# Second mixer of a two-block transformer: global heads first, then banded heads, with panels and half of the output projection between the attention's steps

## The chip, the cores and the metric

One core of one Trainium2 chip. The metric is the device time of one execution in microseconds. TensorE (PE), VectorE (DVE), ScalarE (ACT), GpSimd (POOL) and the load queue of SyncE (SP) run their own instruction streams in order and meet at semaphores.

## The reference

Two transformer blocks on 512 tokens of width 1024, in fp32. The change concerns the mixer of the second block:

```python
h = rms_norm(x, norm_mix_pre[l])
qa, ka, va, qb, kb, vb = jnp.split(h @ w_in[l], SPLITS, axis=-1)
qa = apply_rope(rms_norm(qa.reshape(B, S, 8, 64), q_norm_a[l]), ang_axial)
ka = apply_rope(rms_norm(ka.reshape(B, S, 2, 64), k_norm_a[l]), ang_axial)
out_a = global_attention(qa, ka, va)          # all 512 keys
qb, kb = apply_rope(qb, ang_1d), apply_rope(kb, ang_1d)
out_b = window_attention(qb, kb, vb, sink_b[l])   # |key - query| <= 128, one sink logit per head
mixed = jnp.concatenate([rms_norm(out_a, group_norm_a[l]),
                         rms_norm(out_b, group_norm_b[l])], axis=-1) @ w_out[l]
x = x + rms_norm(mixed, norm_mix_post[l])
```

Eight global heads (a) share two key heads, eight banded heads (b) likewise.

## The kernel before

Activations lie transposed, features on partitions and 512 tokens in the free dimension. Each fp32 product is made of three matmuls of rounded parts: high by high, low by high, high by low (lines 710 to 712). A weight **unit** is a 128 x 1024 panel: SyncE loads it into one of four raw slots, GpSimd splits it into high and low part (`split`, lines 595 and 597) in one of two slots, TensorE uses it in eight **chunks** of three matmuls. A split waits until the unit two before it is used up (`unit_done`).

The second mixer, in TensorE's order:
- twelve panels (units U_B2) for keys, queries and values, a and b by turns. Query panels hold head j and head j + 4 of their kind. Between their chunks stand, for a: the fp32 sum of squares per head (`sum_a`, line 808), then VectorE's `head_norm` (reciprocal L1917, scaling L1919), the fp32 rotation (`turn_a`, L811), VectorE's `rope` (L1925 multiply, L1929, L1932 add), and high and low part; for b the rotation alone. The factor of the norm over all features, `r_all`, multiplies the panels' results.
- attention over 16 heads, in pairs a, a, b, b. A step is one key block of 128: an a head has four, a b head four and one for the sink. For each step `scores_t` makes transposed scores plus the shift by the row maximum (L856 to L864), ScalarE takes exponentials twice, GpSimd makes the low part of the probabilities (L632), and two steps later `values_mm` adds to the output (L885 to L887). Row maxima come from a second set of scores (`scores`, L841), which TensorE makes for head h + 1 during steps 0 and 1 of head h; VectorE's `maxes` (L1949) reads them, and in step 2 `diagonal` (L1963, for b after L1959) writes the shift as four diagonal matrices. `output` (L1978, L1981) divides a pair's result one step after ScalarE has copied it out.
- `w_out_2`: eight units of the output projection, each for 128 output features, over all eight chunks c of the normalized heads; chunks 0 to 3 are a, 4 to 7 b, in two banks. The two group norms' factors are taken afterwards, in `join` (L2437, L2440, L2442). GpSimd's splits go on ahead; during the attention GpSimd makes only low parts.

Banks: two for scores, three for transposed scores, two for outputs. During `fox_slot`, in the first block's mixer (580 to 740 us of the span), another attention stands chunk by chunk between panels, with one bank for scores and two for transposed scores.

## Time and profile before

| | us |
|---|---|
| median of 3 runs | 2176.59 |
| lowest, highest | 2175.07, 2177.75 |
| the profiled execution | 2175.67 |
| its span | 2173.6 |
| TensorE busy | 2004.6 |
| GpSimd busy | 1226.0 |
| VectorE busy | 1105.3 |
| ScalarE busy | 505.0 |

Times below are microseconds from the start of the span. The busy time of TensorE counts each matmul to its modelled end, and matmuls overlap, so the distance of their starts is the better measure of work. A wait in the trace is put down to the releaser that came last.

### The profile page before, as it was taken

What the parts mean: (1) busy time and instruction counts of PE and PEld (TensorE: products, weight loads), DVE (VectorE), ACT (ScalarE), POOL (GpSimd) and SP (SyncE); (2) the same over time, 40 slices, a digit from 0 to 9 for tenths busy, and PEclk for the clock granted to TensorE, in tenths of its full rate; (3) what the DMA queues carried; (4) which work ended last, traced back from release to release, by engine and by line L of the source; (5) the groups of instructions that cost most, each with busy time, mean ns of one, the idle gap of its engine ahead of it and who ended that gap; (6) DMA issues with size and microseconds to landing.
All of it is one profiled execution on the core that took longest, in us unless ns stands there. A gap on an engine that the chain in (4) does not pass through costs nothing.

```text
span 2173.6 us, 25282 instructions
## 1 busy us (share of the span) xinstructions
PE 2004.6 (92%) x8955; PEld 1623.3 (75%) x8955; DVE 1105.3 (51%) x1308; ACT 505.0 (23%) x916; POOL 1226.0 (56%) x752
## 2 busy tenths in 40 slices
PE   7999999789989899889999999998888869999996
PEld 5888888467767687678778888876676748888884
DVE  5333430557676467666653332039778684333104
ACT  3111100344334342350111110022365321111001
POOL 4666666336645545436666666664445456666661
PEclk9999999889999999999999999999999979999998
DMA  4333323212211223102323333233100113333220
GB/s 150 97 97 96 97 96 88 78 49 78 68 49 50 59 59 87 49 1 83 92 88 96 96 96 98 96 90 84 49 0 1 39 49 97 96 96 96 97 87 39
DMA packets 259808, 163.83 MB, mean 75 GB/s; under 512 B 30380, under 2 KB 249582, under 8 KB 259614
## 3 DMA queue, kind: packets, MB, share of 16 engines
q1 hardware_dynamic: 258080, 157.90, 24.8%
q10 hardware_dynamic: 1662, 5.06, 0.7%
q8 instruction: 41, 0.67, 0.1%
q14 instruction: 25, 0.20, 0.0%
HBM read 160.81 MB, written 2.13 MB: 75 GB/s over the span
## 4 chain that ended last, share of the span: by engine, by line
PE 77%; DVE 14%; ACT 3%; issue 2%; POOL 2%; ACTq 1%; DMA 0%; POOLq 0%; DVEq 0%; SPq 0%
PE bank L710 12%; PE bank L711 12%; PE bank L712 12%; PE bank L778 5%; PE bank L777 5%; PE bank L779 5%; PE bank L971 3%; PE bank L972 3%; PE bank L973 3%; DVE work L1978 2%; PE bank L841 2%; DVE work L1917 1%; PE bank L1176 1%; PE bank L1177 1%; PE bank L1178 1%
## 5 line engine op out<-in xcount | busy, mean ns | idle before, releaser
L597 POOL TENSOR_TENSOR w_lo<-raw,w_hi 128x1024 fp32r<-128x1024 f32 x298 | 746.1, 2504 | 24.9
L595 POOL TENSOR_SCALAR w_hi<-raw 128x1024 fp32r<-128x1024 f32 x298 | 320.5, 1075 | 711.9 <-PE bank L712 340.9
L710 PE MATMUL bank<-u_hi,w_hi 128*128 128x512 f32 x1184 | 476.3, 402 | 28.8 <-DVE u_lo L1866 19.1
L711 PE MATMUL bank<-u_lo,w_hi 128*128 128x512 f32 x1184 | 465.4, 393 | 0.0
L712 PE MATMUL bank<-u_hi,w_lo 128*128 128x512 f32 x1184 | 465.0, 393 | 0.0
L710 PEld LDWEIGHTS bank<-u_hi,w_hi 128*128 128x128 f32 x1184 | 224.6, 190 | 91.3 <-issue 25.5
L711 PEld LDWEIGHTS bank<-u_lo,w_hi 128*128 128x128 f32 x1184 | 225.0, 190 | 49.5 <-issue 4.7
L712 PEld LDWEIGHTS bank<-u_hi,w_lo 128*128 128x128 f32 x1184 | 224.9, 190 | 47.1
L1892 DVE TENSOR_TENSOR work<-bank,work 128x512 f32<-128x512 f32 x66 | 45.6, 691 | 285.1 <-PE bank L712 285.1
L779 PE MATMUL bank<-hid_hi,w_lo 128*128 (+1 forms) x480 | 186.9, 389 | 0.0
L778 PE MATMUL bank<-hid_lo,w_hi 128*128 (+1 forms) x480 | 186.9, 389 | 0.0
L777 PE MATMUL bank<-hid_hi,w_hi 128*128 (+1 forms) x480 | 186.9, 389 | 0.0
L971 PE MATMUL bank<-u_hi,w_hi 128*128 128x512 f32 x384 | 158.3, 412 | 2.4 <-ACT work L1328 1.1
L1897 DVE TENSOR_TENSOR hid_lo<-work,hid_hi 128x512 f32 (+1 forms) x66 | 123.1, 1865 | 59.4 <-ACT hid_hi L1365 59.4
L972 PE MATMUL bank<-u_lo,w_hi 128*128 128x512 f32 x384 | 151.5, 395 | 0.0
L973 PE MATMUL bank<-u_hi,w_lo 128*128 128x512 f32 x384 | 151.4, 394 | 0.0
L1365 ACT ACTIVATE hid_hi<-work 128x512 f32 (+1 forms) x66 | 41.8, 633 | 360.2 <-DVE work L1895 360.2
L1949 DVE TENSOR_REDUCE rowmax<-bank 128x1 f32<-128x512 f32 (+3 forms) x144 | 72.7, 525 | 90.4 <-PE bank L841 89.6
L632 POOL TENSOR_TENSOR p_pl<-work,p_ph 128x512 fp32r<-128x512 f32 (+2 forms) x64 | 73.4, 1157 | 70.4 <-ACT work L1416 70.3
L1912 DVE SCALAR_TENSOR_TENSOR hT<-bank,hT 128x512 f32<-128x512 f32 x16 | 11.0, 688 | 199.2 <-PE bank L800 199.2
L777 PEld LDWEIGHTS bank<-hid_hi,w_hi 128*128 128x128 f32 x480 | 90.2, 188 | 18.8
L779 PEld LDWEIGHTS bank<-hid_hi,w_lo 128*128 128x128 f32 x480 | 90.2, 188 | 18.6
(463 smaller groups left out, 3293.7 us busy)
## 6 DMA issues: line engine op xcount, KB each, us to landing
raw<-in_w_in SPq DMA_DIRECT2D x52, 512.0 KB, 3.7
raw<-in_ffn_w_gate SPq DMA_DIRECT2D x44, 512.0 KB, 3.8
raw<-in_ffn_w_up SPq DMA_DIRECT2D x44, 512.0 KB, 3.7
raw<-in_ffn_w_down SPq DMA_DIRECT2D x44, 512.0 KB, 3.5
raw<-in_w_gate SPq DMA_DIRECT2D x22, 512.0 KB, 3.7
raw<-in_w_up SPq DMA_DIRECT2D x22, 512.0 KB, 3.7
raw<-in_w_down SPq DMA_DIRECT2D x22, 512.0 KB, 3.7
raw<-in_w_branch SPq DMA_DIRECT2D x12, 512.0 KB, 3.4
```

The lines of the kernel that those rows point to most:

```text
L595: pool.tensor_scalar(w_hi[:, s, :], raw[:, k, :], 1.0, 1.0, ALU.mult, ALU.mult).then_inc(hi_done, 1)
L597: pool.tensor_tensor(w_lo[:, s, :], raw[:, k, :], w_hi[:, s, :].bitcast(F32), ALU.subtract).then_inc(split_ready, 1)
L710: pe.matmul(outs[:, 0:n], wh, rhs_hi[:, c, :], start=(c == 0), stop=False)
L711: pe.matmul(outs[:, 0:n], wh, rhs_lo[:, c, :], start=False, stop=False)
L712: last = pe.matmul(outs[:, 0:n], wl, rhs_hi[:, c, :], start=False, stop=(c == KC - 1))
L777: pe.matmul(bank[m][:], wh, hid_hi[:, j, :], start=start, stop=False)
L778: pe.matmul(bank[m][:], wh, hid_lo[:, j, :], start=False, stop=False)
L779: last = pe.matmul(bank[m][:], wl, hid_hi[:, j, :], start=False, stop=stop)
L971: pe.matmul(o, wh, rhs_hi[:, c, :], start=(c == 0), stop=False)
L972: pe.matmul(o, wh, rhs_lo[:, c, :], start=False, stop=False)
L973: last = pe.matmul(o, wl, rhs_hi[:, c, :], start=False, stop=(c == KC - 1))
L1897: dve.tensor_tensor(hid_lo[:, f, :], W[8 + k], hid_hi[:, f, :].bitcast(F32), ALU.subtract).then_inc(f_lo, 1)
```

## The change

- Order: `b2_heads` now holds the eight a heads, then the eight b heads, so o2T's chunk g is pair g.
- Panels stand in the order of B2_PANELS. Six (ka, qa0, va, qa1, kb, qa2) come before the attention, six (qa3, qb0, qb1, vb, qb2, qb3) are **fillers**: a generator gives one chunk at a time, four between head 0's scores, then five per head.
- The output projection's units cover 256 output features of one group. The four of group a (A_HALF, 32 chunks) are fillers too, the four of group b (`w_out_b`) follow the attention. VectorE's `half_out` multiplies the first half by its group's factor during the attention; `join` adds the second.
- Scores have one bank, transposed scores two, banks 4 and 5 serve the fillers, bank 1 the turns and sums (AUX). Maxima move to steps 1 and 2, the diagonal to step 3.
- Norms, turns and low parts of the later heads are put at fixed steps of the loop (`hooks` on TensorE, `later` on VectorE and ScalarE). ScalarE makes two extra square roots inside it, each followed by `load_exp`.
- Low parts of the probabilities get three rotating places (`prob_lo`) for four fixed ones. GpSimd splits ten units between them.

Tables, orders and the splits:

```diff
+B2_PANELS = "ka", "qa0", "va", "qa1", "kb", "qa2", "qa3", "qb0", "qb1", "vb", "qb2", "qb3"
+B2_BANK = dict(zip(B2_PANELS, (2, 3, 4, 5, 4, 5, 4, 5, 4, 5, 4, 5)))
+B2_AHEAD = 6
...
+        b2_ph = at("b2_ph", [P, TT * S], b2a, F32R)
+        b2a += 8192
+        prob_lo = at("prob_lo", [P, 3, S], work_at + 7 * 2048, F32R)
+        for st in (ast, bst):
+            st |= {"ph": b2_ph, "pl": None, "off": SPREAD}
...
+        S_ORDER = "va", "ka", "qa0", "qa1", "kb", "qa2", "qa3", "qb0", "qb1", "vb", "qb2", "qb3"
+        ROPE_ORDER = "a0", "a1", "a2", "b0", "a3", "a4", "b1", "b2", "b3", "b4"
...
+        B2_BANKS = (0,), (2, 3), (6, 7), None
+        FIRST_FILL = 4
+
+        A_HALF = [(m, c) for m in range(2) for c in range(3)] + [(0, 3), (1, 3)]
+        A_HALF += [(m, c) for m in range(2, KC) for c in range(4)]
+
+        def fill_step(k):
+
+            head, i = (k - FIRST_FILL) // 5, (0, 1, 1, 2, 2)[(k - FIRST_FILL) % 5]
+            return (4 * head if head < 8 else 32 + 5 * (head - 8)) + i
...
-            low_parts(A_B2, b2_heads)
-            for u in range(U_WO2 + SPL, U_GU3 + SPL):
+            emptied = {fill_step(KC * k + KC - 1): U_B2 + B2_AHEAD + k for k in range(10)}
+            for x, step in enumerate(b2_steps):
+                if step[2] is not None:
+                    low_part(A_B2, b2_heads, step)
+                if x in emptied:
+                    one(emptied[x] + SPL)
+            for u in range(U_WO2 + 4 + SPL, U_GU3 + SPL):
...
         b2_heads = []
         for j in range(4):
             for job in pair(ast, whole, q=qa2[j]):
-                b2_heads.append(job | {"q_ready": S_B2 + (LAST_A if j == 3 else 2 * j + 3) + 1, "v_ready": S_B2 + V_A + 1})
+                b2_heads.append(job | {"q_ready": s_no(f"qa{j}") + 1, "v_ready": s_no("va") + 1})
+        for j in range(4):
             for job in pair(bst, window, q=qb2[j], extra=lambda *a, j=j: band(qb2[j][0], *a), extra_t=band_t, sinks=j):
-                b2_heads.append(job | {"q_ready": S_B2 + (LAST_B if j == 3 else 2 * j + 2) + 1, "v_ready": S_B2 + V_B + 1})
+                b2_heads.append(job | {"q_ready": s_no(f"qb{j}") + 1, "v_ready": s_no("vb") + 1})
         b2_steps = steps_of(b2_heads)
         b2_ends = [last_step(b2_steps, 2 * g + 1) for g in range(KC)]
```

TensorE:

```diff
...
-                for p in range(4, 12):
-                    j = (p - 4) // 2
-                    if p % 2 == 0:
-                        pe.wait_ge(qa_raw, j + 1)
-                    else:
-                        pe.wait_ge(r_raw, RR_B2 + j + 1)
-                    panel(u + p, p % SPL, 2 + p % 4, U, hooks(p))
-                attend(A_B2, b2_heads, part="rest", hooks={
-                    3: lambda: (pe.wait_ge(r_out, R_B2 + 10), values(VR_B2 + 1, 5, W[1]))})
...
+            def out_mm(b, slot, m, c, hi):
+                j, o = c % 4, bank[b][:]
+                a = j * 2 * P + m % 2 * P
+                pe.matmul(o, w_hi[:, slot, a:a + P], hi[:, j, :], start=j == 0, stop=False)
+                pe.matmul(o, w_hi[:, slot, a:a + P], ou_lo[:, c, :], start=False, stop=False)
+                return pe.matmul(o, w_lo[:, slot, a:a + P], hi[:, j, :], start=False, stop=j == 3)
+
+            def fillers():
+
...
+                for name in B2_PANELS[B2_AHEAD:]:
+                    for c in b2_panel(name):
+                        yield
+                        if c == 0:
+                            bank_free(name)
+                for m, c in A_HALF:
+                    yield
+                    u = U_WO2 + m // 2
+                    if c == 0:
+                        pe.wait_ge(split_ready, u + 1)
...
+                    pe.wait_ge(g_lo, c + 1)
+                    last = out_mm(Q_BANK + m % 2, u % SPL, m, c, oua_hi)
+                    if c == 3:
+                        last.then_inc(unit_done if m % 2 else g_half, 1)
+
...
+                for c in b2_panel("qa1"):
+                    if c == 2:
+                        sum_a(0, 6)
+                    if c == 5:
+                        pe.wait_ge(h_std, H_B2 + 1)
+                        sum_a(1, 6)
+                pe.wait_ge(v_raw, VR_B2 + 1)
+                for c in b2_panel("kb"):
+                    if c == 1:
+                        pe.wait_ge(qa_raw, 1)
+                        values(VR_B2, 2, W[0])
+                    if c == 4:
+                        turn_a(0, 7)
+                    if c == 6:
+                        pe.wait_ge(h_std, H_B2 + 2)
+                        sum_a(2, 6)
+                pe.wait_ge(qa_raw, 3)
+                for c in b2_panel("qa2"):
+                    if c == 6:
+                        pe.wait_ge(r_out, rope_no("a0") + 1)
+                        turn_a(1, 7)
+                fill = fillers()
+                next(fill)
+                scores, scores_t, values_mm = attention(A_B2, b2_heads, B2_BANKS)
+                for qt in range(TT):
+                    scores(0, qt)
+                    go_on(fill, 1)
+                    if qt == 0:
+                        pe.wait_ge(h_std, H_B2 + 3)
+                        sum_a(3, 6)
...
+                hooks = {
+                    2: lambda: (pe.wait_ge(h_std, H_B2 + 4), turn_a(2)),
+                    3: lambda: aux_free("a2", lambda: turn_b(0)),
+                    5: lambda: aux_free("b0", lambda: turn_a(3)),
+                    9: lambda: aux_free("a3", lambda: sum_a(4, AUX)),
+                    13: lambda: turn_a(4),
+                    17: lambda: aux_free("a4", lambda: turn_b(1)),
+                    20: lambda: aux_free("b1", lambda: turn_b(2)),
+                    27: values_b,
+                    32: lambda: (pe.wait_ge(s_lo, s_no("vb") + 1), turn_b(3)),
+                    40: group_sum_a,
+                    44: lambda: (pe.wait_ge(g_std, 1), turn_b(4)),
+                }
+                for x, (h, i, kb, t, b) in enumerate(b2_steps):
+                    if x in hooks:
+                        hooks[x]()
+                    scores_t(h, i, kb, t)
+                    more = h + 1 < len(b2_heads) and i in (1, 2)
+                    if i <= 2:
+                        go_on(fill, 1)
+                    if more:
+                        scores(h + 1, 2 * i - 2)
+                    if x >= PV_LAG and b2_steps[x - PV_LAG][2] is not None:
+                        h_, i_, kb_, t_, b_ = b2_steps[x - PV_LAG]
+                        values_mm(h_, i_, kb_, b_)
+                    if i in (1, 2):
+                        go_on(fill, 1)
+                    if more:
+                        scores(h + 1, 2 * i - 1)
+                for h, i, kb, t, b in b2_steps[-PV_LAG:]:
+                    if kb is not None:
+                        values_mm(h, i, kb, b)
+                for _ in fill:
...
+                for c in range(4, 7):
+                    pe.wait_ge(g_lo, c + 1)
+                    for m in range(4):
+                        out_mm(banks[m], (u + m // 2) % SPL, m, c, oub_hi)
+                pe.wait_ge(g_lo, 8)
+                for m in range(4):
+                    out_mm(banks[m], (u + m // 2) % SPL, m, 7, oub_hi).then_inc(unit_done if m % 2 else g_half, 1)
+                    if m == 1:
+                        pe.wait_ge(a_o, A_B2[3] + 16)
+                        pe.wait_ge(g_add, 6)
+                        pe.matmul(bank[6][:], ones, raw_x[:, 0, :], start=True, stop=True).then_inc(g_sum, 1)
+                for m in range(4, KC):
+                    v = u + m // 2
+                    pe.wait_ge(split_ready, v + 1)
+                    if m >= 6:
+                        pe.wait_ge(g_part, KC + m - 5)
+                    for c in range(4, 8):
+                        last = out_mm(banks[m], v % SPL, m, c, oub_hi)
+                    last.then_inc(unit_done if m % 2 else g_half, 1)
+                sum_total(N_POST, 7)
+            w_out_b()
```

VectorE:

```diff
...
                 raw_a_of(0)
+                raw_a_of(1)
+                raw_v_of(0)
+                norm_a(0)
+                raw_a_of(2)
+                value_low(s_no("va"), ast, 2)
                 dve.wait_ge(ld_tab, 16)
...
+                turn_a(0, 7)
+                norm_a(1)
+                low_a(0)
+                scale_tables()
+                turn_a(1, 7)
+                low_a(1)
+                raw_a_of(3)
...
+                def half_out(m):
+                    if m % 2:
+                        dve.wait_ge(unit_done, U_WO2 + m // 2 + 1)
...
+                    dve.tensor_tensor(mo[:, m, :], bank[Q_BANK + m % 2][:], W[0], ALU.mult).then_inc(g_part, 1)
+                first = {b2_ends[g] + PV_LAG + 6: [lambda g=g: group_low(g)] for g in range(KC - 1)}
+                later = {
+                    0: [lambda: norm_a(2)],
+                    2: [lambda: turn_a(2)],
+                    3: [lambda: (low_a(2), dve.wait_ge(tab_scaled, 1), turn_b(0))],
+                    4: [lambda: norm_a(3)],
+                    6: [lambda: (low_b(0), turn_a(3), raw_a_of(4))],
+                    8: [lambda: low_a(3)],
+                    12: [lambda: norm_a(4)],
+                    14: [lambda: turn_a(4)],
+                    16: [lambda: low_a(4)],
+                    17: [lambda: turn_b(1)],
+                    18: [lambda: low_b(1)],
+                    20: [lambda: turn_b(2)],
+                    22: [lambda: low_b(2)],
+                    25: [lambda: raw_v_of(1)],
+                    28: [lambda: value_low(s_no("vb"), bst, AUX)],
+                    33: [lambda: turn_b(3)],
+                    36: [lambda: low_b(3)],
+                    41: [lambda: factor(0)],
+                    45: [lambda: turn_b(4)],
+                    47: [lambda: low_b(4)],
+                }
+                for m in range(KC):
+                    x = fill_step(KC * (len(B2_PANELS) - B2_AHEAD) + A_HALF.index((m, 3))) + 1
+                    first.setdefault(max(42, x), []).append(lambda m=m: half_out(m))
+                maxes, diagonal, output = attention(A_B2, b2_heads, lambda r, g: o2T[r, g, :], B2_BANKS)
+                for qt in range(TT):
+                    maxes(0, qt)
+                diagonal(0)
+                for x in range(len(b2_steps) + PV_LAG + 3):
+                    h, i = b2_steps[x][:2] if x < len(b2_steps) else (len(b2_heads), 0)
+                    for step in first.get(x, []):
+                        step()
+                    if h + 1 < len(b2_heads) and i in (1, 2):
+                        maxes(h + 1, 2 * i - 2)
+                        maxes(h + 1, 2 * i - 1)
+                    if h + 1 < len(b2_heads) and i == 3:
+                        diagonal(h + 1)
+                    if x - PV_LAG - 2 in b2_ends:
+                        output(b2_ends.index(x - PV_LAG - 2))
+                    for step in later.get(x, []):
+                        step()
                 group_low(KC - 1)
+                factor(1)
```

## Rows read from the trace of the kernel before

**Rows 1.** The page, part 1: busy time, share of the span, instructions of each engine.

```profile
PE 2004.6 (92%) x8955; PEld 1623.3 (75%) x8955; DVE 1105.3 (51%) x1308; ACT 505.0 (23%) x916; POOL 1226.0 (56%) x752
```

**Rows 2.** Busy time of each engine by stage (columns: PE, PEld, DVE, ACT, POOL, clock).

```profile
580.00:740.00 160.00, 145.46 (x683) 115.48 (x684) 102.75 (x120) 62.30 (x126) 85.42 (x67) 0.97 0.18 48
...
1551.00:1701.00 150.00, 128.41 (x667) 106.75 (x666) 112.09 (x167) 91.35 (x188) 76.81 (x66) 0.98 0.01 4
1701.00:1752.00 51.00, 47.60 (x196) 37.47 (x196) 39.92 (x35) 8.95 (x15) 24.89 (x15) 0.97 0.23 68
1752.00:1767.00 15.00, 2.08 (x2) 0.50 (x2) 10.88 (x9) 2.60 (x5) 5.77 (x4) 0.58 0.18 52
1767.00:1785.00 18.00, 13.36 (x26) 7.82 (x27) 17.45 (x18) 8.64 (x15) 10.69 (x7) 0.50 0.00 1
```

**Rows 3.** Timeline of TensorE: start and end of the loop, end of the projection.

```profile
1551.51 0.39 PE L856 MATMUL bank<-q2ah,a_k0h 128*128 128x512 f32 x1
...
1700.09 0.39 PE L889 MATMUL bank<-b_k1h,zero_r 128*128 128x512 f32 x1
...
1750.89 0.39 PE L1282 MATMUL bank<-ou_hi,w_lo 128*128 128x512 f32 x1
```

**Rows 4.** Waits of TensorE, 1551 to 1701 (waiter, releaser: us, times, longest).

```profile
PE bank L841 <- DVE rowmax L1949: 7.9, 6, 1.4
...
PE bank L885 <- POOL p_pl L632: 5.3, 7, 1.1
...
PE bank L864 <- DVE shift L1963: 3.0, 2, 1.5
PE bank L884 <- POOL p_pl L632: 2.7, 1, 2.7
```

**Rows 5.** Waits of TensorE, 580 to 740, attention of the first mixer.

```profile
PE bank L856 <- ACT work L1416: 4.5, 3, 1.7
PE bank L808 <- ACT work L1378: 4.4, 1, 4.4
...
PE bank L841 <- DVE rowmax L1949: 3.6, 7, 0.6
```

**Rows 6.** Timeline of TensorE: an fp32 sum and the chunks behind it.

```profile
1479.15 1.12 PE L808 MATMUL bank<-work,const 128*128 128x512 f32 x2 [2.15 <-ACT work L1768]
...
1480.35 0.40 PE L711 MATMUL bank<-u_lo,w_hi 128*128 128x512 f32 x1
...
1482.41 0.39 PE L711 MATMUL bank<-u_lo,w_hi 128*128 128x512 f32 x1
```

**Rows 7.** Operations on the raw heads of the projection (ns, min/median/max).

```profile
L1919 DVE SCALAR_TENSOR_TENSOR raw_a<-raw_a,gain,work x5: 750/752/2058, 1486.3 to 1539.6; 128x512 f32<-128x512 f32 x5
L1925 DVE TENSOR_TENSOR raw_a<-raw_a,tab x5: 686/1524/2760, 1491.2 to 1555.8; 128x512 f32<-128x512 f32 x5
L1932 DVE TENSOR_TENSOR raw_a<-raw_a,turn_tmp x5: 692/986/2085, 1492.6 to 1557.9; 128x512 f32<-128x512 f32 x5
```

**Rows 8.** Groups of VectorE, 1551 to 1701 (busy us, mean ns, idle before).

```profile
L1978 DVE RECIPROCAL work<-work 128x512 f32<-128x512 f32 x7 | 23.5, 3353 | 7.2 <-ACT work L1427 7.1
L1949 DVE TENSOR_REDUCE rowmax<-bank 128x1 f32<-128x512 f32 x28 | 18.0, 685 | 7.9 <-PE bank L841 7.9
...
L1959 DVE TENSOR_SCALAR negmax<-rowmax,sink 128x4 f32<-128x4 f32 x8 | 6.7, 837 | 0.2
```

**Rows 9.** Timeline of VectorE: four diagonals beside GpSimd, and alone.

```profile
1584.40 1.62 DVE L1963 TENSOR_SCALAR shift<-const,rowmax 128x128 fp32r<-128x128 f32 x4
...
1610.88 0.88 DVE L1963 TENSOR_SCALAR shift<-const,negmax 128x128 fp32r<-128x128 f32 x4
```

**Rows 10.** Timeline of VectorE: the factor r_all, the last low part, last squares.

```profile
1474.43 3.29 DVE L1842 RECIPROCAL work<-work 128x512 f32<-128x512 f32 x1
...
1707.93 0.75 DVE L2419 SCALAR_TENSOR_TENSOR ou_lo<-o2T,gain,ou_hi 128x512 fp32r<-128x512 f32 x1 [1.38 <-ACT turn_tmp L1811]
...
1755.40 1.47 DVE L1877 TENSOR_TENSOR work<-work 128x512 f32<-128x512 f32 x2
```

**Rows 11.** Groups of GpSimd, 1445 to 1560.

```profile
L597 POOL TENSOR_TENSOR w_lo<-raw,w_hi 128x1024 fp32r<-128x1024 f32 x14 | 36.1, 2581 | 1.2
```

More of the change, by code:

```diff
@@ L254, in two_blocks @@
         tab_scaled, qa_raw, g_part = sem("tab_scaled"), sem("qa_raw"), sem("g_part")
+        g_sq, g_add, g_sum, g_std, g_rec, g_hi, g_lo, g_half = (
+            sem("g_" + n) for n in ("sq", "add", "sum", "std", "rec", "hi", "lo", "half"))
         c_two, g_raw = sem("c_two"), sem("g_raw")
@@ L1220, in first_key, with turn_a, turn_b, sum_a @@
+            def turn_a(a, b=AUX):
+                pe.wait_ge(h_out, H_B2 + a + 1)
+                rotate(b, raw_x[:, X_OF[a], :])
+            def turn_b(j):
+                pe.wait_ge(r_raw, RR_B2 + j + 1)
+                rotate(AUX, raw_x[:, 2 + j % 2, :])
+            def sum_a(a, b):
+                head_sum(H_B2 + a, b, HEAD_SQ[a], blk64)
+            def mixer_in():
                 def first_key(c):
@@ new lines, in mixer_in @@
+                exps, output = attention(A_B2, b2_heads, lambda r, g: o2T[r, g, :], B2_BANKS)
+                ends = {last_step(b2_steps, h): h for h in range(len(b2_heads))}
+                for x in range(len(b2_steps) + PV_LAG + 1):
+                    if x in first:
+                        group_high(first[x])
+                    if x < len(b2_steps):
+                        exps(*b2_steps[x])
+                    if x in later:
+                        later[x]()
+                    if x - PV_LAG - 1 in ends:
+                        output(ends[x - PV_LAG - 1])
@@ L2391, in mixer_in @@
-                last.then_inc(tab_scaled, 1)
-                raw_a_of(1)
-                norm_a(0)
-                dve.wait_ge(tab_scaled, 1)
-                turn_b(0)
-                dve.wait_ge(h_out, H_B2 + 1)
-                turn_a(0)
-                low_b(0)
-                for j in range(1, 5):
-                    norm_a(j)
-                    if j < 4:
-                        raw_a_of(j + 1)
-                    else:
-                        raw_v_of(0)
-                    turn_b(j)
-                    low_a(j - 1)
-                    dve.wait_ge(h_out, H_B2 + j + 1)
-                    if j < 4:
-                        turn_a(j)
-                        low_b(j)
@@ L2425, in mixer_in @@
-                attend(A_B2, b2_heads, put, part="first")
-                hooks = {b2_ends[g] + PV_LAG + 6: lambda g=g: group_low(g) for g in range(KC - 1)}
-                hooks |= {0: lambda: value_low(S_B2 + V_A, ast, 6), 1: lambda: raw_v_of(1), 2: lambda: turn_a(4),
-                          3: lambda: (low_b(4), low_a(4)), 5: lambda: value_low(S_B2 + V_B, bst, 5)}
-                attend(A_B2, b2_heads, put, part="rest", hooks=hooks)
+                raw_a_of(1)
+                raw_v_of(0)
```

405 lines of the change are left out of this document (211 added, 194 removed).

## The prediction

> **What bounds the kernel now.** The page gives TensorE 92% of the span [rows 1]. The stage table comes next, because the change touches only 1453 to 1757: twelve panels of the second mixer's projection until 1551, then the attention loop, then the output projection [rows 2]. In the loop TensorE is called 128.4 us busy of 150 and VectorE 112.1; in the projection TensorE is 47.6 of 51. Landmarks: the loop's first transposed score starts at 1551.51, its last matmul at 1700.09, so it ends near 1700.3; the last projection matmul starts at 1750.89 [rows 3]. The loop is 148.8 us long. Its waits on TensorE come to 18.9 us, 12.7% of it: row maxima, the low parts of the probabilities, the shift [rows 4]. So TensorE bounds the stage, with VectorE close behind and handshakes between them. What interleaving could win is those waits, plus what the panel stage loses. VectorE's 112.1 of 150 us limit the win.
>
> **Work that moves.** Matmuls of 512 columns follow each other every 0.228 us (nine from 1480.35 to 1482.41), so one chunk (three matmuls) is 0.68 us; an fp32 sum or turn between them takes 1.20 - 0.23, about 0.9 us [rows 6]. No matmul is added or removed: 96 panel chunks, 64 output chunks, the same attention. Into the loop move 76 chunks (48 of panels and 32 of the output's first half, less four issued just before it), 51.8 us, and ten sums and turns, 9 us (turn_a(2) to (4), sum_a(4), turn_b(0) to (4), the group sum). The old loop without its waits and without the 2% that a clock of 0.98 cost [rows 2] is 148.8 - 18.9 - 3 = 127 us, its small handshakes included. New loop: 127 + 52 + 9 = 188 us of TensorE work.
>
> **Its start.** Until the factor r_all (reciprocal from 1474.43, 3.29 us: 1477.7 [rows 10]) nothing changes. From there VectorE sets the pace: three products (1.8) and the wait for the first root, 1480.8; norm_a(0), a reciprocal and a scaling (3.35 + 0.75, the scaling up to 2.06 [rows 7, 8]), 1484.9; raw_a_of(2) behind panel qa1, 1486.4; value_low behind its transposes, 1488.6; turn_a(0), 1492.0; norm_a(1), 1496.1; low_a(0) and the tables 2.7 to 4, turn_a(1) 2.0, its high and low part 1.3: about 1503. Head 0's four scores, four chunks and a sum take 5.5: the loop starts at 1508.5 (within 1.5), 43 us earlier than before.
>
> **Waits in the new loop.** Four edits make it tighter. Maxima are taken at i = 1 and 2 and the diagonal at i = 3, before at 0, 1 and 2: between the last score of the next head and the matmul that needs its shift TensorE now has two short steps, 2.3 us. The scores have one bank for two. The hooks put a norm (4.1 us), turns and low parts between maxima, and three TensorE hooks wait for just these. In the banded half an output factor (sum, reciprocal, product: 0.6 + 3.4 + 0.6 at the pace at which they follow each other) falls at i = 2, ahead of the diagonal. VectorE's pieces: a 512-wide maximum 0.69 and a head's reciprocal 3.35, the negated maxima 0.84 with what they wait for [rows 8]; four diagonals 0.88 alone, 1.62 beside GpSimd [rows 9]; a turn 2.0 alone, to 3.5 when its multiply and add meet GpSimd (686 to 2760 ns, 692 to 2085 [rows 7]).
> One place in full, step 13. VectorE takes the last maximum 0.7 after its score; at step 11 it makes the diagonal (1.0) and output(0) (4.0), at 12 norm_a(4) (4.1): 9.8 us after the score. TensorE has 1.6 of work at step 11 and 2.3 at step 12, then turn_a(4) asks for the norm: it idles 5.9 us, 7 if the scaling meets GpSimd. Counted likewise in order: step 1, 1.6 to 2; step 3 (turn_b(0) behind turn_a(2)) 2.7 to 3.4; step 5 (turn_a(3) behind low_a(2), which waits for ScalarE, and norm_a(3)) 4 to 5.5; step 8 (shift behind low_b(0), turn_a(3), raw_a_of(4)) 3.2 to 5; step 16, 2.1 to 3.4; steps 21, 24 and 32, 2.2 to 5.6. Global half: 22 to 32 us. Banded half: three times 0.45 + 4.6 + 0.5 to 1.2 + 0.9 to 1.6 against 2.3, 12 to 17 us; steps 41 to 43 (root and table load, factor(0), half_out) 1 to 3; the other diagonals 0 to 3. In all 36 to 55 us. I take 40, near the lower end, since the 127 above already hold the usual handshakes. The loop is then 228 us and ends at 1736.5.
>
> **Low parts and splits.** GpSimd needs about 3.5 us for a split (the low part alone 2.58 [rows 11]); ten of them now stand between low parts of probabilities. Each chunk group lasts 8/5 of a head, over 17 us, so a split is ready in time; a low part behind it is 1.3 us late at worst, and the products lag two steps. Nothing is taken for it; exposed each time it is 10 x 1.3. The queue of loads (SyncE) is filled long before: no cost. ScalarE's extra copies lie in its idle time.
> At this place the Trainium skill speaks, "SBUF — State Buffer", section "Who interferes with whom": a VectorE instruction with two SBUF inputs and a GpSimd one that reads SBUF exclude each other for a whole instruction. The trace agrees with it, 686 against 2760 ns for one multiply [rows 7]; by that rule alone the upper ends above would be the usual case and the loop 15 us longer.
>
> **The tail.** Before: 1700.3 to the last square's sum, 1755.40 + 1.47 = 1756.9 [rows 10]: 56.6 us. After: twelve chunks (8.2 us) cover the last head's factor, whose low part starts 7.6 us after the last matmul and ends 8.4 after it [rows 10]; then two chunks 1.4, sum 0.9, root 0.6, reciprocal 3.4: 14.8. Eight joins with square sums of 1.9 us each, 15.5, and some 4 us of meeting GpSimd's four splits: 34.5 us (31 to 40). VectorE, not TensorE (24 us), bounds it. Gain 22.1 us. What follows (root, residual, next feed-forward, at a clock of 0.5 [rows 2]) is the same.
> Sum against the profiled execution's 2175.7 us: break-even is a loop end of 1756.9 - 34.5 = 1722.4. 1736.5 is 14.1 us later: 2189.8. The median of the runs, 2176.6, stands 0.9 above the profiled one, so 2190 to the full microsecond. I forecast slower, 2190, own range 2182 to 2198.
>
> **Rivals.**
> (1) No change. If TensorE waits the same share as before, 12.7%, the loop is 188/0.873 = 215 us and ends at 1723.8: 2177. For it: VectorE's busy share hardly changes (75% before; after, 112.1 and some 43 of moved operations, 155 of 228: 68%). Against it: the counted queues.
> (2) Faster: the chunks fill the waits. Between 580 and 740 the first mixer's attention runs interleaved with panels in the same way, one score bank included, and TensorE waits there for 12.5 of 160 us in its three largest rows, 7.8% [rows 5], only 3.6 of it for row maxima. At that share the loop is 204 us and ends at 1712.4: 2166. It decides from a wait sum below 22 us. Against it: there two thirds of TensorE's time are panels, here under a third, and its hooks ask for fewer results that are just being made.
> The Trainium skill's "Perfetto Trace Analysis" has rules for both sides. "Optimization Strategy" says that interleaving regimes with different bottlenecks may help: that is rival (2). "Matmuls" says that independent groups should rotate through PSUM banks; the change takes one from the scores and one from the transposed scores. By rows 5 the price of a single bank is small.
> (3) Much slower: GpSimd is met nearly always, the waits reach their upper end of 55 us: loop 243 us, 2205. Longer gaps could also bring the clock down: it was granted at 0.58 from 1752 to 1767, where TensorE was 2.1 us busy of 15, and at 0.50 (1.2 GHz) after it [rows 2]. For it: low parts of probabilities and splits together keep GpSimd busy most of the time.
> (4) It doesn't interleave: chunks wait for their splits, ten times 3.5 us more: 2225.
>
> **Chances.** Forecast 0.50, (1) 0.17, (2) 0.18, (3) 0.12, (4) 0.03. 0.2% is 4.4 us, about what a measurement tells from no change. Faster: rival (2) and the edge of (1), 0.21; same 0.17; slower 0.62. The range 2163 to 2206 takes in most of (2), all of (1) and (3).
>
> **What would show it.** In the profile after: loop start near 1508.5; its end near 1736 (below 1722 I am wrong in sign); TensorE's waits in it 36 to 55 us, the longest at turns of the global half behind L1919's and L1925's results and at the shift every second banded head; tail of 34 us with VectorE busy throughout; panel waits for w_lo near zero. A wait sum under 25 us would mean that VectorE's queue is shorter than I counted.

## The result and the profile after

The changed kernel takes 2231.8 us (2229.8 to 2232.3, four runs), the kernel before beside it 2177.1: ratio 1.0251 [1.0233, 1.0269], 54.7 us slower. The direction was forecast, the size was not: 2190, range 2163 to 2206. The profiled execution took 2231.8 us; its span is 2229.8 us.

The page of after, part 1, answers [rows 1]: the same matmuls, a little less VectorE.

```profile
PE 2024.4 (91%) x8955; PEld 1639.8 (74%) x8955; DVE 1084.6 (49%) x1308; ACT 512.3 (23%) x923; POOL 1222.9 (55%) x752
```

Busy time by stage of after (columns as in [rows 2], of which these are the counterpart): the panels ahead of the loop, four scores of head 0, the loop in three parts (the banded half begins at 1650.3, inside the second), then two parts of the tail.

```profile
1453.00:1505.00 52.00, 40.36 (x161) 29.15 (x160) 45.13 (x49) 13.17 (x23) 27.41 (x15) 0.98 0.37 91
1505.00:1513.00 8.00, 7.00 (x18) 4.40 (x19) 3.85 (x6) 2.71 (x4) 0.14 (x1) 0.71 0.31 66
1513.00:1600.00 87.00, 61.24 (x204) 44.70 (x203) 49.41 (x64) 30.32 (x53) 33.93 (x23) 0.83 0.07 19
1600.00:1666.00 66.00, 58.59 (x270) 47.01 (x269) 41.33 (x64) 31.25 (x60) 34.34 (x25) 0.99 0.06 16
1666.00:1776.00 110.00, 89.02 (x443) 78.20 (x444) 55.31 (x87) 42.92 (x92) 37.98 (x36) 0.86 0.09 25
1776.00:1803.00 27.00, 22.75 (x96) 17.48 (x94) 21.96 (x18) 6.56 (x11) 12.98 (x8) 1.00 0.20 58
1803.00:1813.00 10.00, 0.79 (x1) 0.50 (x2) 8.94 (x12) 2.52 (x4) 1.42 (x1) 0.51 0.18 53
```

The column to read is the one behind POOL: the clock granted to TensorE. Before, it was 0.98 over the loop [rows 2]; now it is 0.83 in the loop's first part and 0.86 in its third, which lies in the banded half. In the middle part, where the clock is 0.99, TensorE is also 89% busy.

Waits of TensorE in the loop of after (waiter, releaser: us, times, longest), the counterpart of [rows 4]:

```profile
PE bank L895 <- DVE shift L2121: 29.4, 10, 4.6
PE bank L842 <- DVE raw_x L2077: 12.0, 2, 6.2
PE bank L842 <- DVE raw_x L2090: 4.3, 1, 4.3
PE bank L887 <- ACT work L1528: 3.2, 2, 1.7
PE bank L872 <- DVE rowmax L2107: 2.4, 3, 1.3
PE bank L1237 <- issue: 1.9, 1, 1.9
PE bank L916 <- POOL prob_lo L658: 0.9, 2, 0.6
```

54.1 us, of which 45.7 us at the shift and at the turns, where the prediction had put them. The loop starts at 1513.0 and its last matmul at 1775.1 (in this execution r_all is 1.0 us later than in that of before). The last square's sum of the tail ends at 1812.15:

```profile
1810.67 1.48 DVE L2035 TENSOR_TENSOR work<-work 128x512 f32<-128x512 f32 x2
```

**Where the time went.** I split each loop into three: its waits on TensorE, the time lost at half clock (over short equal stretches, TensorE's busy time times one minus the granted clock), and the rest, which is work.

| us | before | after | difference |
|---|---|---|---|
| first transposed score | 1551.5 | 1513.0 | -38.5 |
| work in the loop | 125.6 | 183.4 | +57.8 |
| waits of TensorE in it | 20.1 | 54.1 | +34.0 |
| lost at half clock in it | 2.9 | 24.6 | +21.7 |
| last attention matmul to last square's sum | 56.8 | 37.0 | -19.8 |
| sum | 1756.9 | 1812.1 | +55.2 |

The moved work (57.8) costs what the earlier start and the shorter tail give back (58.3). So the change could win only by filling waits, and the loop before had 20 us of them. Instead the waits grew by 34 us, and the loss at half clock by another 22.

### The profile page after: what moved, and what is told of

Its sections match the earlier page's. It is cut to its first block, busy times and chain, and to the rows that moved or that the text cites. A ratio compares the mean times of both kernels' runs of the same rounds, so it can differ in the third digit from the quotient of the medians.

```text
span 2229.8 us, 25288 instructions
## 1 busy us (share of the span) xinstructions
PE 2024.4 (91%) x8955; PEld 1639.8 (74%) x8955; DVE 1084.6 (49%) x1308; ACT 512.3 (23%) x923; POOL 1222.9 (55%) x752
## 4 chain that ended last, share of the span: by engine, by line
PE 78%; DVE 13%; issue 3%; ACT 2%; POOL 2%; ACTq 1%; DMA 0%; POOLq 0%; DVEq 0%; SPq 0%
PE bank L741 12%; PE bank L743 12%; PE bank L742 12%; PE bank L809 5%; PE bank L808 5%; PE bank L810 5%; PE bank L1002 4%; PE bank L1003 4%; PE bank L1004 4%; PE bank L872 2%; DVE work L2136 2%; DVE work L2075 1%; PE bank L1207 1%; PE bank L1209 1%; PE bank L1208 1%
## 5 line engine op out<-in xcount | busy, mean ns | idle before, releaser
L741 PEld LDWEIGHTS bank<-u_hi,w_hi 128*128 128x128 f32 x1088 | 206.5, 190 | 79.8 <-issue 21.4
L743 PEld LDWEIGHTS bank<-u_hi,w_lo 128*128 128x128 f32 x1088 | 206.6, 190 | 43.4
L742 PEld LDWEIGHTS bank<-u_lo,w_hi 128*128 128x128 f32 x1088 | 206.9, 190 | 42.7 <-issue 0.7
L658 POOL TENSOR_TENSOR prob_lo<-work,b_ph 128x512 fp32r<-128x512 f32 (+2 forms) x64 | 71.5, 1118 | 161.6 <-ACT work L1539 161.6
L1002 PEld LDWEIGHTS bank<-u_hi,w_hi 128*128 128x128 f32 x480 | 92.1, 192 | 26.3 <-issue 6.4
L1004 PEld LDWEIGHTS bank<-u_hi,w_lo 128*128 128x128 f32 x480 | 91.4, 191 | 20.4
```

What stands on the lines that cost most here:

```text
L741: pe.matmul(outs[:, 0:n], wh, rhs_hi[:, c, :], start=(c == 0), stop=False)
L742: pe.matmul(outs[:, 0:n], wh, rhs_lo[:, c, :], start=False, stop=False)
L743: last = pe.matmul(outs[:, 0:n], wl, rhs_hi[:, c, :], start=False, stop=(c == KC - 1))
L1002: pe.matmul(o, wh, rhs_hi[:, c, :], start=(c == 0), stop=False)
L1004: last = pe.matmul(o, wl, rhs_hi[:, c, :], start=False, stop=(c == KC - 1))
```

## Experiments

Ratios are against the kernel before, run beside each. The last three columns are of the profiled execution's loop, split as above.

| kernel | median us | ratio and interval | loop | waits | half clock |
|---|---|---|---|---|---|
| after | 2231.8 | 1.0251 [1.0233, 1.0269] | 262.1 | 54.1 | 24.6 |
| e1 zeros in the waits | 2219.8 | 1.0194 [1.0177, 1.0211] | 251.2 | 31.4 | 8.3 |
| e2 output later | 2235.5 | 1.0263 [1.0245, 1.0280] | 264.9 | 56.8 | 26.2 |
| e2b and ScalarE's queue | 2229.7 | 1.0248 [1.0231, 1.0265] | 261.9 | 53.0 | 27.2 |
| e3 global half spread | 2214.1 | 1.0174 [1.0157, 1.0191] | 244.2 | 47.2 | 12.7 |
| e4 both | 2207.4 | 1.0139 [1.0122, 1.0156] | 238.3 | 41.7 | 12.9 |
| e5 both, zeros | 2205.9 | 1.0131 [1.0114, 1.0148] | 236.7 | 30.5 | 8.3 |
| e11 after, no division | 2214.1 | 1.0178 [1.0163, 1.0194] | 245.4 | 43.7 | 18.6 |
| e13 both, no division | 2195.3 | 1.0084 [1.0069, 1.0100] | 224.0 | 31.8 | 9.2 |
| e12 before, no division | 2162.2 | 0.9937 [0.9922, 0.9953] | 136.3 | 12.4 | 0.4 |
| e7 before, late maxima | 2181.3 | 1.0019 [1.0009, 1.0029] | 159.1 | 23.3 | 12.4 |
| e8 e7 with fewer banks | 2214.7 | 1.0172 [1.0155, 1.0189] | 183.7 | 40.6 | 16.4 |
| e9 before, zeros | 2171.0 | 0.9979 [0.9970, 0.9988] | 148.3 | 19.9 | 3.4 |

The split can be trusted to about a microsecond: loop less waits less half clock is 182 to 184 us in all kernels of the changed order without zeros, although their loops differ by 41 us. The length of the stretches moves the half clock of a kernel by up to about a microsecond.

### The clock: zeros in the waits (e1)

```diff
+        IDLE = {2: 10, 4: 14, 6: 8, 11: 24, 13: 28, 15: 24}
...
                     if i == 0:
+                        for k in range(IDLE.get(h, 0) if done is A_B2 else 0):
+                            pe.matmul(o, zero_r[:], job["k"][0][:, 0:n], start=False, stop=False)
                         pe.wait_ge(a_shift, h0 + h + 1)
```

and likewise 14, 18 and 20 of them ahead of the turns at steps 3, 5 and 13.

> The changed kernel with matmuls against a block of zeros placed ahead of nine of its longest waits on TensorE (shift of heads 2, 4, 6, 11, 13 and 15; the turns at steps 3, 5 and 13). They add zero to a sum that is open or fill a bank that is written anew, 160 matmuls in all, at most as many as the wait held, and leave every result as it was. Theory A (the waits are as counted, and each wait of 3 to 6 us also brings the granted clock to 0.5 for some us of the work behind it): the stretches at 0.5 behind these waits go, the loop falls from 262 to about 244 us, the time from 2231.8 to 2212 to 2220. Rival B (the clock falls in stretches in which nothing waits for TensorE's pace): 2230 to 2234, the clock higher and the time the same. Rival C (the filling matmuls are in the way of what follows, clock unchanged): 2234 to 2245.

Measured 2219.8, 12 us less; the loop is 10.9 us shorter. What it does is seen at the turn of step 3. Timeline of TensorE in after (start, duration; in brackets the idle time and what ended it):

```profile
1527.94 2.08 PE L842 MATMUL bank<-raw_x,const 128*128 128x512 f32 x2 [4.33 <-DVE raw_x L2090]
...
1530.24 0.63 PE L891 MATMUL bank<-q2l,a_k0h 128*128 128x512 f32 x1
1530.67 0.63 PE L892 MATMUL bank<-q2h,a_k0l 128*128 128x512 f32 x1
1531.10 0.63 PE L895 MATMUL bank<-shift,ones_r 128*128 128x512 f32 x1
```

and in e1:

```profile
1523.87 3.33 PE L1338 MATMUL bank<-u_hi,zero_r 128*128 128x512 f32 x14
1528.40 1.12 PE L843 MATMUL bank<-raw_x,const 128*128 128x512 f32 x2 [1.20 <-DVE raw_x L2101]
...
1529.59 0.40 PE L892 MATMUL bank<-q2l,a_k0h 128*128 128x512 f32 x1
1529.83 0.39 PE L893 MATMUL bank<-q2h,a_k0l 128*128 128x512 f32 x1
1530.06 0.39 PE L898 MATMUL bank<-shift,ones_r 128*128 128x512 f32 x1
```

After the idle 4.33 us the same matmuls follow each other every 0.43 us, at a granted clock of 0.50 (1.2 GHz); behind the zeros every 0.23 us, at 1.00. Over the loop the loss at half clock falls from 24.6 to 8.3 us, and 11 of these 16 us arrive in the time. Theory A holds, though for the loop it had expected 244 us and 251.2 came; B and C fall.

### VectorE's order (e2, e2b, e3, e4)

e2 puts the output factor behind the diagonal in the banded half:

```diff
-                    if x - PV_LAG - 2 in b2_ends:
-                        output(b2_ends.index(x - PV_LAG - 2))
+                    done = x - PV_LAG - (3 if x > 36 else 2)
+                    if done in b2_ends:
+                        output(b2_ends.index(done))
```

> The changed kernel with one edit on VectorE: in the banded half the output factor (sum, reciprocal, product, 4.6 us) stands one step later, behind the diagonal and not ahead of it. Theory A (the queue of VectorE between the last maximum and the shift is what TensorE waits for at heads 11, 13 and 15): the three waits of 3.9 to 4.5 us at the shift fall below 1 us each, with the half clock behind them some 12 to 16 us: 2216 to 2221. If only the waits go and the clock stays: 2221 to 2223. Rival (the output factor is late next, at the sink or at the group's low part, and takes the waits over): 2228 to 2232.

Measured 2235.5, 2.6 us more by the ratios, which is inside the uncertainty: no gain where theory A had 11 to 16 us. The rival is right in kind, since the waits move to the sink, though the time lies above its range. The shift's waits fall, from 29.4 to 17.2 us, and TensorE waits 18.9 us for the sink's exponential instead. The largest of these, 7.4 us, in the timeline of e2:

```profile
1701.49 0.69 DVE L2139 TENSOR_TENSOR o2T<-o2T,work 128x512 f32<-128x512 f32 x1
...
1704.22 0.63 ACT L1430 ACTIVATE q2h<-raw_x 128x512 fp32r<-128x512 f32 x1 [7.64 <-DVE raw_x L2090]
1704.76 0.70 ACT L1934 ACTIVATE oub_hi<-o2T,gain 128x512 fp32r<-128x512 f32 x1
...
1705.89 0.67 ACT L1528 ACTIVATE work<-bank,sink 64x512 f32<-64x512 f32 x1
...
1706.61 0.69 PE L887 MATMUL bank<-q2h,b_k1h 128*128 128x384 f32 x1 [7.41 <-ACT work L1528]
```

ScalarE is in order too: the high part of a query pair stands there waiting for the turn, which VectorE now makes after the output factor, and the exponential that frees TensorE's bank stands behind it. So e2b moves ScalarE's items as well:

```diff
-                first = {b2_ends[g] + PV_LAG + 4: g for g in range(KC - 1)}
+                first = {b2_ends[g] + PV_LAG + (5 if g > 3 else 4): g for g in range(KC - 1)}
...
-                    45: lambda: high_b(4),
+                    49: lambda: high_b(4),
...
-                    45: [lambda: turn_b(4)],
-                    47: [lambda: low_b(4)],
+                    47: [lambda: turn_b(4)],
+                    50: [lambda: low_b(4)],
```

> The output factor of the banded half behind the diagonal as in the kernel with the output later, and now ScalarE's queue goes with it: the group's high part one step later, so that it stands behind the sink's exponential and not ahead of it, and turn, high and low part of the last query pair moved away from that step. Theory A': the 7.4 us waits at the transposed score behind the sink's exponential, which took the place of the shift's waits, came from ScalarE's order (high parts waiting for VectorE ahead of the exponential); without them the three waits at the shift and their half clock are gone: 2214 to 2222. Rival (VectorE's work per head in the banded half is itself as long as TensorE's, whatever the order): 2228 to 2233, with the same sum of waits at other lines.

Measured 2229.7: within the measurement of after, waits 53.0 for 54.1, now 10.5 us of them at row maxima. The rival's number came, but not its reason: VectorE is busy 64.6 us of the 123 of this half (1651 to 1774), so its work is not as long as TensorE's. What the trace of e2b shows is its order again. With one bank the next head's second score waits for the maximum of its first, and that maximum now stands behind the output factor, the turn, a low part and half_out:

```profile
1695.96 0.68 DVE L2132 TENSOR_TENSOR work<-work 128x512 f32<-128x512 f32 x1
1696.67 3.35 DVE L2136 RECIPROCAL work<-work 128x512 f32<-128x512 f32 x1
...
1704.44 0.41 DVE L2107 TENSOR_REDUCE rowmax<-bank 128x1 f32<-128x256 f32 x1
...
1704.91 0.44 PE L872 MATMUL bank<-b_k0h,q2h 128*128 128x384 f32 x1 [4.10 <-DVE rowmax L2107]
```

e3 does the same for the global half. In VectorE's dictionary (TensorE's and ScalarE's follow it):

```diff
-                    3: [lambda: (low_a(2), dve.wait_ge(tab_scaled, 1), turn_b(0))],
-                    4: [lambda: norm_a(3)],
-                    6: [lambda: (low_b(0), turn_a(3), raw_a_of(4))],
-                    8: [lambda: low_a(3)],
-                    12: [lambda: norm_a(4)],
-                    14: [lambda: turn_a(4)],
...
+                    4: [lambda: (low_a(2), dve.wait_ge(tab_scaled, 1), turn_b(0))],
+                    5: [lambda: raw_a_of(4)],
+                    7: [lambda: norm_a(3)],
+                    8: [lambda: low_b(0)],
+                    9: [lambda: turn_a(3)],
+                    12: [lambda: low_a(3)],
+                    15: [lambda: norm_a(4)],
+                    17: [lambda: turn_a(4)],
...
```

> The changed kernel with the norms, turns and low parts of the global half at other steps: the turns that TensorE asks for come later (steps 4, 9, 17, 20 and 24 for 3, 5, 13, 17 and 20), norms and low parts stand behind the diagonal instead of ahead of a maximum or diagonal, the group's low parts too. No work is added or removed. Theory A (the waits of the global half, 4.3, 5.9, 3.6, 6.2, 4.6 and 3.1 us, are those of the places where results are asked for too soon): half of the 32 us of waits and some 8 us of half clock go, 2205 to 2215. Rival (VectorE is 90% full in these 87 us by my count of its work, so that the waits only change place): 2224 to 2234.

The group's low parts also move, from ahead of the maxima to behind the diagonal. Measured 2214.1, 17 us less by the ratios, inside theory A's range, but made up otherwise: only 7 us of waits went, and 12 us of half clock. The long waits became short ones. The waits at the turns, 16.3 us in three places in after, are 6.8 in three in e3:

```profile
PE bank L872 <- DVE rowmax L2108: 6.0, 6, 1.8
PE bank L895 <- DVE shift L2122: 5.4, 3, 3.2
PE bank L842 <- DVE raw_x L2078: 4.1, 2, 2.2
PE bank L1237 <- issue: 3.5, 1, 3.5
PE bank L842 <- DVE raw_x L2091: 2.7, 1, 2.7
```

(waits of TensorE in e3, 1513 to 1660). e4 is e3 with e2b's edits:

> Both together: global half spread and banded half with output and ScalarE's queue later. Theory A: the gains add, 2190 to 2203, still slower than before, since 10 to 20 us of waits and clock, the matmul work moved and the tail balance remain. Rival: one of the two only changes the place of the waits, then the time is that of the other alone.

Measured 2207.4, 24 us below after, but above the 2190 to 2203 that theory A gave: once the global half is spread, the banded half's edit is worth 7.6 us, alone it was worth nothing that can be measured. Why it is worth more here no run separates. It stays 30 us above before. The largest row of its 41.7 us of waits is now that of the row maxima:

```profile
PE bank L872 <- DVE rowmax L2108: 10.0, 8, 3.3
PE bank L895 <- DVE shift L2122: 8.2, 5, 3.3
```

### VectorE's load (e11, e12, e13)

These three leave out the division by the softmax sum, so they give times and no right results:

```diff
-                    dve.reciprocal(inverse, den).then_inc(a_rec, 1)
+                    if done is A_B2:
+                        dve.tensor_scalar(inverse, den, 1.0 / S, None, ALU.mult).then_inc(a_rec, 1)
...
```

for the eight output factors of this attention alone.

> The changed kernel with the eight reciprocals of the second mixer's attention outputs (3.35 us each on VectorE) replaced by a multiplication with 1/512, some 0.6 us: the division by the softmax sum is left out, so this measures time only. It takes 22 us of work from VectorE in the loop and changes no order. Theory A'' (after the experiments on order: VectorE's load between maximum and shift is the bound, not order alone): the waits at shift and turn fall by 12 to 18 us and the half clock behind them by 6 to 10: 2204 to 2215. Rival (the order alone, the reciprocals mostly lie where TensorE has other work): 2222 to 2230.

> The kernel before with the same reciprocals left out (same part of the computation missing). Its loop waits 19 us, 8.5 of them for row maxima, and VectorE is 75% busy. Theory A'': the queue there has room, 3 to 8 us: 2168 to 2174. If it falls as much as the changed kernel, VectorE's load explains nothing of the difference between the two.

> The changed kernel with both halves spread (2207.4) and the same reciprocals left out. Theory A'': order and load are two views of one queue, so what is left is 22 us less on VectorE for some 10 to 15 us of time: 2190 to 2197, and the waits on VectorE below 10 us in all. If the changed order then stands level with the kernel before without its reciprocals (2168 to 2174), VectorE is the whole difference; I expect 15 to 25 us to be left, from the clock and the waits for ScalarE, GpSimd and panels.

Measured 2214.1, 2162.2 and 2195.3: less by 16 (after), 14 (before) and 12 us (e4) by the ratios. I expected 3 to 8 for the kernel before and was wrong. The divisions are on the path of both kernels, so their load is no reason for the difference: that is 52 us without them, 55 with them. The norms, turns and low parts that moved into the loop are load too, and no run leaves them out; that where they stand matters is shown by e3 and e4, for 24 of the 55 us. In e13 the waits for VectorE were to be below 10 us and are 25.4, and it stays 33 us above e12 where I had expected 15 to 25: this remainder is not explained.

### The schedule and the banks by themselves (e7, e8)

In the kernel before, scores and maxima of the next head at steps 1 and 2 and the diagonal at step 3, for this attention:

```diff
-                    if h + 1 < len(heads) and i < TT // 2:
-                        maxes(h + 1, 2 * i)
-                        maxes(h + 1, 2 * i + 1)
+                    at = i - 1 if done is A_B2 else i
+                    if h + 1 < len(heads) and 0 <= at < TT // 2:
+                        maxes(h + 1, 2 * at)
+                        maxes(h + 1, 2 * at + 1)
...
```

> The kernel before with the tighter schedule of the second mixer's attention alone: scores and maxima of the next head at steps 1 and 2, the diagonal at step 3; order of heads, banks, panels and projection as before. Theory A: heads of four steps have two short steps between last score and shift, output(g) falls at step 2 or 3 ahead of or behind the diagonal; waits grow by 10 to 20 us in the loop of 149, the time 2187 to 2200. Rival D (the tighter schedule costs nothing by itself, the waits of the changed kernel come from the moved norms and turns alone): 2175 to 2180.

Measured 2181.3 over ten runs, ratio 1.0019 [1.0009, 1.0029]: some 4 us, neither theory's number. Its runs spread more than before's, from 2178.2 at a mean clock of 0.968 to 2190.7 at 0.962; the profile is that last one, so its row in the table shows the upper end, and its factor r_all is already 3.0 us later than in the profile of before (1477.48 for 1474.43), ahead of anything the edit touches.

e8 adds the banks: `FEW = (0,), (2, 3), (6, 7), None` in place of `USUAL`.

> The same with the changed kernel's banks for this attention as well: one for scores instead of two, two for transposed scores instead of three. Theory A: the bank costs little by itself, 0 to 6 us more than the kernel with the late maxima alone. Rival B2 (the missing banks are a main cause): 15 us more or beyond.

Measured 2214.7, 33 us more than e7; I had expected 0 to 6, and the rival's "15 us more or beyond" came. The largest row of its waits is one that is small in after (TensorE's waits in e8's loop):

```profile
PE bank L842 <- DVE rowmax L1951: 25.4, 30, 3.0
```

With one bank, each score waits for the maximum of the one before. In after there is a chunk or a product between two scores, and the same wait is 2.4 us in 3 places. So the price is real, but in after the chunks fill all but these 2.4 us. It is not gone for good: in e2b and e4 the row maxima hold 10.5 and 10.0 us. The changed order with a second bank for scores was not run. On this the Trainium skill, "Perfetto Trace Analysis", section "Matmuls", says that independent groups should rotate through PSUM banks; e8's 25.4 us agree with it, after's 2.4 show that other work between the groups can do as well.

### What kept clock is worth elsewhere (e9, e5)

e9 is the kernel before with 20 zero matmuls ahead of head 0's scores, 7 in the projection's first unit, 28 ahead of the last sum and 48, then 8 each, in the next feed-forward's first panel:

```diff
+            def keep_on(n, b=7):
+                for k in range(n):
+                    pe.matmul(bank[b][:, 0:3 * P], zero_r[:], masks_r[:].rearrange("p a n -> p (a n)")[:, 0:3 * P],
+                              start=b == 7, stop=b == 7)
...
-                        at_c[5] = lambda: (pe.wait_ge(r_out, R_B2 + 9), attend(A_B2, b2_heads, part="first"))
+                        at_c[5] = lambda: (keep_on(20, 5), pe.wait_ge(r_out, R_B2 + 9), attend(A_B2, b2_heads, part="first"))
```

> The kernel before with matmuls against a block of zeros in four of its waits: ahead of the first scores in the last panel (20), in the last wait of the projection's first unit (7), ahead of the last sum (28) and between the chunks of the next feed-forward's first panel (48, then 8 each). They go to an open sum as zeros or to an unused bank. The clock is 0.5 from 1546 to 1550, 0.6 to 0.9 from 1707 to 1714 and 0.5 from 1754 to 1785 in the profile of before; TensorE works little there until 1782, so that at most 2 + 2 + 2 us are to be had: 2170 to 2175. Rival: the clock rises and the time stays within 1 us of before, since VectorE sets the pace of the tail.

Measured 2171.0 (eleven runs), 0.9979 [0.9970, 0.9988]: faster than both kernels, by 4.6 us against before. The loop starts at 1548.0 instead of 1551.5, but 1.95 of these 3.5 us are there before the first zero matmul (at 1538.7): r_all's reciprocal starts at 1472.48 for 1474.43. That leaves some 1.6 us of the start to the zeros; how the rest of the 4.6 us divides among the places was not tested. Same stretch, kernel before and then e9 (columns as in [rows 2]):

```profile
1542.00:1548.00 6.00, 2.99 (x7) 1.97 (x8) 5.60 (x11) 0.00 (x0) 0.00 (x0) 0.84 0.30 87
1548.00:1552.00 4.00, 4.00 (x16) 2.61 (x16) 0.96 (x5) 0.66 (x2) 0.14 (x1) 0.81 0.01 4
```

```profile
1542.00:1548.00 6.00, 5.27 (x22) 3.28 (x21) 4.33 (x10) 0.49 (x2) 0.00 (x0) 1.00 0.15 43
1548.00:1552.00 4.00, 4.00 (x17) 2.74 (x15) 3.39 (x7) 2.98 (x6) 3.55 (x3) 1.00 0.00 0
```

e5 adds zeros to e4 at seven places of the loop and in the tail:

> Both halves spread (2207.4) with matmuls against zeros in eight of its remaining waits and in the tail (12, 8 and 8 ahead of the turns at steps 4, 9 and 17, 14 ahead of the group sum, 12, 12 and 16 ahead of the shift of heads 4, 8 and 11; 28 ahead of the last sum and 48 and 8 each between the chunks of the next feed-forward's first panel). Theory A: of the 13 us that half clock costs in this loop and the 2 to 4 in the tail some 8 to 11 come back: 2196 to 2200. Rival (what is left is waits for VectorE, the clock in them costs nothing): 2205 to 2208. In either case it stays above the kernel before, whose stage has 19 us of waits in a loop with two banks for scores.

Measured 2205.9, 1.7 us less than e4 by the ratios, inside the uncertainty. The half clock in the loop falls by 4.6 us and the loop by 1.6 only. The rival's number came, for these waits. Its reason, that VectorE is late anyway and faster matmuls only reach the next wait sooner, fits but was not tested by itself. In e1, whose waits were long, two thirds came back.

## Why the prediction was right or wrong

The direction and the places of the waits were right. Two steps of the sum failed: the clock behind the new waits was put at nothing and took 24.6 us of the loop, and the counted waits of 36 to 55 us were entered as 40 and measured 54.1.

- **Work in the loop, 188 us.** Its 18.9 us of old waits leave out a fifth row of the view of [rows 4], L817 with 1.2 us (20.1 in all), so the 127 was a little high. Measured 183.4; the way of counting (chunks at 0.68, sums and turns at 0.9) holds.
- **Start, 1508.5.** 1513.0, less the 1.0 by which r_all is late: 3.5 us late. The chain on VectorE was 1.8 us late (first score at 1505.8, for 1503 and the 1.0); head 0's four scores with chunks and sum took 7.2 us for my 5.5, at a clock of 0.71 from 1505 to 1513. So about half of the miss lies in the chain and half at the half clock.
- **Waits, 36 to 55, taken 40.** Measured 54.1, at the counted places: step 3, 4.3 (I had up to 3.4); step 5, 5.9 (to 5.5); step 8, 3.6; step 13, 6.2 (5.9 to 7); step 16, 4.6 (to 3.4); the three of the banded half 3.9, 4.5 and 4.0, 12.4 in all (12 to 17). The places were right and the sum lies within the count, at its upper end; at steps 3, 5 and 16 the wait is 0.4 to 1.2 us above my upper bound, for a reason that no run shows. The failed step is the choice: I took 40 "since the 127 above already hold the usual handshakes", a discount for something that the counted queues do not contain. 14 us.
- **GpSimd meeting VectorE.** Milder than the upper ends. Medians in after: the scaling 752 ns, the multiply 684, which reached 1524 before [rows 7]; longest 2376 and 912; the 2376 stands ahead of the loop, at 1495.9 beside GpSimd's w_lo, and no scaling in the loop took more than 0.8 us. The waits reached their upper end without it, so my reason for that end was wrong.

```profile
L2077 DVE SCALAR_TENSOR_TENSOR raw_x<-raw_x,gain,work x5: 751/752/2376, 1485.4 to 1578.2; 128x512 f32<-128x512 f32 x5
L2083 DVE TENSOR_TENSOR raw_x<-raw_x,tab x10: 678/684/912, 1490.5 to 1702.4; 128x512 f32<-128x512 f32 x10
```

  By the rule that I had weighed there, the upper ends would be the usual case (the Trainium skill, "SBUF — State Buffer", "Who interferes with whom"); one instruction of 2376 for 751 ns beside GpSimd agrees with it, but it is not the usual case here.
- **The clock.** The decisive gap: in rival (3) I named it and gave it no price, and the sum took the old loop's 3 us out and put none in. It took 24.6 us in the loop, by the split; e1, which removed 16 of them, got 11 back in time, so not all of it is to be had. I had the rows to price it: the stretch of 15 us at 0.58 in [rows 2] shows that it falls when TensorE idles. I took it as a matter of the tail and did not put it on waits of 4 to 6 us, of which the old loop had none (its longest was 2.7 [rows 4]). The Trainium skill, "TensorE: Matmul & The Clock Gate", describes a kernel whose waits for transfers bring the clock down again and again ("HAM oscillation — how this bites in real kernels"); the half clock behind after's waits, which are for VectorE, agrees with it.
- **Tail, 34.5 us (31 to 40).** 36.8 from the last matmul's end: right, with VectorE busy 8.9 of the last 10 us. Three instructions took 2.9, 2.1 and 1.5 us beside GpSimd's splits for 0.7 alone, together 4.4 us more: my "some 4 us of meeting".
- **Splits.** 0: TensorE has no wait for w_lo above a microsecond in after's loop. Right.
- **Sum.** 2189.8 + 3.5 (start) + 14.1 (waits) + 24.6 (clock) - 4.6 (work) + 2.3 (tail) + 1.0 (r_all) = 2230.7, for 2231.8 measured. (The forecast itself adds 0.9 for the median to 2189.8, which is 2190.7; its 2190 is rounded down.)
- **Rivals.** (2) fell: chunks fill the waits for row maxima (2.4 us, where e8 without chunks has 25.4; "the price of a single bank is small" holds only with chunks between the scores), but not those at shift and turns, which are longer than the chunks placed there. (3) is nearest, 2205, with waits of 55 as it said; its cause, GpSimd met nearly always, was not there, and the clock had no price in it.

**Open.** After e4 the excess over before is 31 us in the profiles: 22 of waits, 10 of half clock. What part of it goes back to the order of the heads (most of the norms and turns of the loop now fall into the eight global heads) was not tried, nor was a second bank for scores. No version of the changed order reached the kernel before.

## What to carry to other kernels

Before interleaving, balance it: here the earlier start and the shorter tail were worth exactly the work moved, so all the profit had to come from waits, and there were only 20 us of them. Count a wait on TensorE by what its releasers have queued ahead of the result, on every in-order engine of the chain (moving VectorE's item alone only handed the wait to ScalarE); take the count as it is, without a discount; and add the half clock behind the long ones (here every wait of 3.6 us or more). Break long waits into short ones by moving the request later, and only then try harmless matmuls against zeros: in e1's long waits they gave 12 us, in e5's short ones nothing measurable.

## What the hardware showed that I had not expected

- Each of the eight waits of 3.6 to 6.2 us in after's loop was followed by 3 to 10 us at a granted clock of 0.5 (1.2 GHz); the one of 3.1 us was not, while four of 1.7 to 2.4 us were. The loop lost 24.6 us at half clock.
- Matmuls with a zero stationary block kept the clock up: 1.00 from 1542 to 1552 in e9, 0.84 and 0.81 before. A matmul of 512 columns starts every 0.23 us at the one level and every 0.43 at the other.
- One program can spread over 12 us (e7, 2178.2 to 2190.7), with the mean clock going from 0.968 to 0.962, while the kernel before beside it stays within 2.5.
